# Turning the latent heads' queries and keys by 32x32 block transposes and transfers instead of on TensorE, with the attention rounds in another order

## The reference, cut to what is computed

```
proj = n @ w_in
c_q, c_kv, k_pe, r_q, r_k, r_v, r_g = split(proj)
q = (rms_norm(c_q) @ w_uq)        # 8 heads x (64 plain + 32 rotated)
kv = (rms_norm(c_kv) @ w_ukv)     # 8 heads x (64 key + 64 value)
s = einsum(q_nope, k_nope) + einsum(rope(q_pe), rope(k_pe))
a = softmax(s * MLA_SCALE) @ v    # latent heads
r = retention_group(r_q, r_k, r_v, r_g)   # decayed scores, no softmax
h = h + concat(a, r) @ w_o
```

## Time and profile before

| | us |
|---|---|
| median of 3 runs | 1026.04 (1025.88 to 1027.49) |
| profiled execution | 1026.88 |
| its span, first to last instruction | 1025.1 |
| TensorE busy | 1015.6 (99%) |
| VectorE busy | 686.6 (67%) |
| ScalarE busy | 564.4 (55%) |
| GpSimd busy | 140.7 (14%) |

### The profile page before, as it was taken

One profiled execution on the slowest core, in us unless ns is written; L12 is line 12 of the kernel. 1 busy time (PEld: TensorE's weight loads), 2 busy tenths in 40 slices (PEclk: granted clock), 3 DMA queues, 4 the chain that ended last, 5 costly groups with the idle time before them and its releaser, 6 DMA issues.

```text
span 1025.1 us, 14271 instructions
## 1 busy us (share of the span) xinstructions
PE 1015.6 (99%) x4764; PEld 836.6 (82%) x4764; DVE 686.6 (67%) x1041; ACT 564.4 (55%) x923; POOL 140.7 (14%) x219
## 2 busy tenths in 40 slices
PE   9999999999999999999999999999999999999997
PEld 6999888888877778888888888888887688888886
DVE  6777865646688985656568565656788785655643
ACT  6665654545567764444556454454676854454542
POOL 1001450000143253000014000000400221000002
PEclk9999999999999999999999999999999999999999
DMA  9574567566643467657576665757653455756551
GB/s 369 187 243 168 195 222 240 183 221 206 207 144 125 145 226 251 224 195 239 180 232 195 231 214 191 244 175 243 200 184 124 146 184 182 245 184 231 195 168 46
DMA packets 109694, 204.61 MB, mean 200 GB/s; under 512 B 57472, under 2 KB 62992, under 8 KB 109648
## 3 DMA queue, kind: packets, MB, share of 16 engines
q1 hardware_dynamic: 107472, 198.55, 57.9%
q0 software_dynamic: 1888, 5.17, 1.6%
q10 hardware_dynamic: 288, 0.31, 0.1%
HBM read 187.20 MB, written 1.05 MB: 184 GB/s over the span
## 4 chain that ended last, share of the span: by engine, by line
PE 93%; DVE 3%; DMA 1%; ACT 1%; SPq 1%; POOL 0%; issue 0%; POOLq 0%; DVEq 0%; ACTq 0%
PE pG L2185 16%; PE pG L2177 16%; PE pG L2181 16%; PE pD L2177 11%; PE pD L2181 11%; PE pD L2185 11%; PE pG L2158 2%; PE pG L2160 1%; PE pG L2164 1%; PE pT L2194 1%; DVE w_low L1735 1%; DMA h<-in_x 1%; PE pD L2158 1%; PE pD L2164 1%; PE pD L2160 1%; PE pT L2379 1%
## 5 line engine op out<-in xcount | busy, mean ns | idle before, releaser
L1735 DVE TENSOR_TENSOR w_low<-raw,w_high 128x1024 fp32r<-128x1024 f32 x339 | 408.9, 1226 | 181.4 <-ACT w_high L1424 171.3
L1424 ACT ACTIVATE w_high<-raw 128x1024 fp32r<-128x1024 f32 x340 | 353.5, 1056 | 192.1 <-PE pG L2185 134.4
L2177 PE MATMUL pG<-w_high,xTh 128*128 128x512 f32 x712 | 219.8, 390 | 0.0
L2185 PE MATMUL pG<-w_low,xTh 128*128 128x512 f32 x712 | 219.4, 389 | 0.2 <-DVE w_low L1735 0.2
L2181 PE MATMUL pG<-w_high,xTl 128*128 128x512 f32 x712 | 219.3, 389 | 0.0
L2185 PEld LDWEIGHTS pG<-w_low,xTh 128*128 128x128 f32 x712 | 133.6, 188 | 28.3 <-DVE w_low L1735 0.6
L2181 PEld LDWEIGHTS pG<-w_high,xTl 128*128 128x128 f32 x712 | 133.5, 188 | 28.0 <-DVE xTl L1795 0.2
L2177 PEld LDWEIGHTS pG<-w_high,xTh 128*128 128x128 f32 x712 | 133.2, 188 | 27.5
L1531 ACT ACTIVATE gate<-pG,stat 128x256 f32<-128x256 f32 x102 | 48.4, 474 | 151.8 <-PE pG L2185 135.9
L2177 PE MATMUL pD<-w_high,aTh 128*128 128x512 f32 x348 | 107.8, 391 | 0.0
L2181 PE MATMUL pD<-w_high,aTl 128*128 128x512 f32 x348 | 107.4, 390 | 0.1
(11 more groups left out here) (318 smaller groups left out, 1113.0 us busy)
## 6 DMA issues: line engine op xcount, KB each, us to landing
raw<-in_stream SPq DMA_DIRECT2D x340, 512.0 KB, 4.3
aF<-aB SPq DMA_DIRECT2D x320, 32.0 KB, 2.5
post<-in_posts POOLq DMA_DIRECT2D x5, 512.0 KB, 5.9
early<-in_stream SPq DMA_DIRECT2D x4, 512.0 KB, 12.5
xF<-hg SPq DMA_DIRECT2D x32, 64.0 KB, 2.5
xF<-hg POOLq DMA_DIRECT2D x32, 64.0 KB, 2.2
h<-in_x SPq DMA_DIRECT2D x2, 512.0 KB, 11.6
first_w<-in_opening SPq DMA_DIRECT2D x2, 384.0 KB, 4.2
```

Source lines behind the costliest of these rows:

```text
L1424: sc.activation(w_high[:, slot(static):slot(static) + CHUNK], raw_of(static), ACT.Copy).then_inc(w_high_done, 1)
L1735: ve.tensor_tensor(w_low[:, slot(static):slot(static) + CHUNK], raw_of(static), w_high[:, slot(static):slot(static) + CHUNK].bitcast(F32), ...
L2177: pe.matmul(dst, ah, w_high[:, where:where + n], start=start, stop=False)
L2185: mm = pe.matmul(dst, ah, w_low[:, where:where + n], start=False, stop=stop)
```

## The change

MT is gone. In its place MB(t) turns 32x32 blocks on VectorE, queries into `post` (free at that time), keys into `mk_turned` (over `junk`), and MV(t) moves them with 8 transfers, 4 from SyncE and 4 from GpSimd. The features of a head are spread over three blocks of 32, and the columns of `w_uq` and `w_ukv` are put in that order on the host. RV(t) is split: queries from SyncE, keys from GpSimd. The first scores stand two chunks later, behind products (3,1,0) and (3,1,1); in a round the order is MS(v), MPT(v-2), ME(v), MN(v-1), one chunk, MPV. Refills of rounds 1 and 3 move to round 7 and behind it.

```
@@ walk_latent
     refill(step, freed, 2)
-    step("MT", 0)
+    step("MB", 0)
+    step("MV", 0)
     refill(step, freed, 2)
     step("KPE", 1)
...
     step("U", 1)
+    step("MB", 1)
+    step("MV", 1)
     step("exp_table",)
     step("RROPE", 1, 0)
     refill(step, freed, 1)
     freed += [C_U, C_U + 1, C_U + 2]
     projects(3, 0, range(2))
-    step("MT", 1)
     refill(step, freed, 1)
     behind_maxima = freed.pop(0) + RING
     step("high", behind_maxima)
     projects(3, 0, range(2, 4))
+    step("RB", 0, 0)
+    project(3, 1, 0)
+    project(3, 1, 1)
     step("MS", 0)
-    step("low", behind_maxima)
     step("ME", 0)
-    step("RB", 0, 0)
-    step("RB", 0, 1)
-    beside = [(3, 1, c) for c in range(4)] + [(4, 0, c) for c in range(4)] + [(4, 1, 0)]
-    project(*beside.pop(0))
-    project(*beside.pop(0))
+    beside = [(3, 1, 2), (3, 1, 3)] + [(4, 0, c) for c in range(4)] + [(4, 1, 0)]
     for v in range(1, 8):
+        step("MS", v)
+        if v >= 2:
+            step("MPT", v - 2)
+        step("ME", v)
         step("MN", v - 1)
-        step("MS", v)
-        if v in (1, 3):
+        if v == 1:
+            step("low", behind_maxima)
+        if v == 7:
             refill(step, freed, 1)
-        step("ME", v)
+        project(*beside.pop(0))
         if v in (3, 5, 7):
             step("MPV", v - 3)
             step("MPV", v - 2)
-        project(*beside.pop(0))
-        step("MPT", v - 1)
         if v == 2:
-            step("VC", 0)
+            step("RB", 0, 1)
+        if v == 3:
+            step("RROPE", 1, 1)
         if v == 4:
             step("RV", 0)
-            step("RROPE", 1, 1)
+            step("VC", 0)
...
         if v == 7:
             step("RV", 1)
-            step("VC", 1)
...
     step("MN", 7)
-    refill(step, freed, 2)
+    step("VC", 1)
+    refill(step, freed, 3)
     project(4, 1, 1)
+    step("MPT", 6)
     step("MPT", 7)
@@ places
-        mqT = place("mqT", [QK, 2, MLA_HEADS, P], F32)
+        mqT = place("mqT", [QK, 2, MLA_HEADS, 4, 32], F32)
-        mkT = place("mkT", [QK, MLA_HEADS, SEQ], F32)
+        mkT = place("mkT", [QK, 2, 4, MLA_HEADS, 32], F32)
@@ SyncE; GpSimd has the same with a in range(2, 4) and m_sent
+            def MV(t, ph):
+                sp.wait_ge(mB_ready, 2 * t + 1)
+                for a in range(0, 2):
+                    sp.dma_start(mqT[:, t, :, a, :], post[32 * a:32 * a + 32, 0:MLA_HEADS * QK]).then_inc(m_moved, 16)
+                sp.wait_ge(mB_ready, 2 * t + 2)
+                for a in range(0, 2):
+                    sp.dma_start(mkT[:, t, a, :, :], mk_turned[32 * a:32 * a + 32, :]).then_inc(m_moved, 16)
@@ SyncE, retention
             def RV(t, ph):
                 sp.wait_ge(ms_psum, 4 * (t + 1))
-                for part in range(2):
-                    sp.wait_ge(rB_ready, 2 * t + part + 1)
-                    for a in range(4):
-                        dst = rkT[:, t, :, a, :] if part else rqT[:, t, a, :, :]
-                        sp.dma_start(dst, block_turned(t, part)[32 * a:32 * a + 32, :]).then_inc(rT_moved[t], 16)
+                if t == 1:
+                    sp.wait_ge(rqT_moved, 64)
+                sp.wait_ge(rB_ready, 2 * t + 1)
+                for a in range(4):
+                    sp.dma_start(rqT[:, t, a, :, :], block_turned(t, 0)[32 * a:32 * a + 32, :]).then_inc(rqT_moved, 16)
@@ VectorE
+            def MB(t, ph):
+                ve.wait_ge(mqk_ready, 2 * t + 2)
+                if t == 1:
+                    ve.wait_ge(m_moved, 64)
+                    ve.wait_ge(m_sent, 64)
+                ve.transpose(post[:, 0:MLA_HEADS * QK], mq[:]).then_inc(mB_ready, 1)
+                ve.wait_ge(u_out, 4 * t + 3)
+                ve.transpose(mk_turned[:], mk[:]).then_inc(mB_ready, 1)
@@ TensorE
                 if v == 0:
-                    for r in range(2):
-                        pe.wait_ge(mqT_ready, 2 * r + 2)
-                        pe.wait_ge(mkT_ready, 2 * r + 2)
+                    pe.wait_ge(m_moved, 128)
+                    pe.wait_ge(m_sent, 128)
+                    pe.wait_ge(u_out, 8)
...
-                    mm = pe.matmul(pG[v % 2][:, SEQ * x:SEQ * (x + 1)], mqT[:, t, hd, :], mkT[:, hd, :],
+                    mm = pe.matmul(pG[v % 2][:, SEQ * x:SEQ * (x + 1)], mqT[:, t, hd, :, :].rearrange("p a j -> p (a j)"), mkT[:, :, :, hd, :],
```

More of the change, by code:

```diff
@@ L1200, in finish @@
                 sp.wait_ge(out_stored, 80)
-            steps = dict(start=start, low=low, low_half=low_half, R=refill, V=V, spread=spread, RV=RV, finish=finish)
+            steps = dict(start=start, low=low, low_half=low_half, R=refill, V=V, spread=spread, MV=MV, RV=RV, finish=finish)
             walk(sp, lambda name, *a, ph=None: steps[name](*a, ph) if name in steps else None)
@@ L1646, in U @@
                     copied(2, 1)
-            def MT(t, ph):
-                sc.wait_ge(mT_psum, 2 * t + 1)
-                for half in range(2):
-                    sc.activation(mqT[:, t, 4 * half:4 * half + 4, :],
-                                  (pG, pT)[half][0][0:QK, :].rearrange("p (a r) -> p a r", a=4), ACT.Copy).then_inc(mqT_ready, 1)
             def ME(v, ph):
@@ L2020, in RB @@
                 ve.wait_ge(rrope_done[t], part + 1)
+                if (t, part) == (0, 0):
+                    ve.wait_ge(mB_ready, 4)
                 ve.transpose(block_turned(t, part), rqk[t][:, 512 * part:512 * part + 512]).then_inc(rB_ready, 1)
@@ L2522, in RS @@
                     pe.wait_ge(mp_ready, 16)
-                    for t in range(2):
-                        pe.wait_ge(rT_moved[t], 128)
+                    pe.wait_ge(rqT_moved, 128)
+                    pe.wait_ge(rkT_moved, 128)
                 else:
@@ L2651, in weight_chunks @@
         if i == 2:
-            parts.extend(np.concatenate([uq[P * k:P * (k + 1)], pad], axis=1) for k in range(2))
-            parts.append(ukv.transpose(0, 2, 1, 3).reshape(P, CHUNK))
+            turned_q = uq.reshape(Q_RANK, MLA_HEADS, 3, 32).transpose(0, 2, 1, 3).reshape(Q_RANK, -1)
+            turned_k = ukv[:, :, 0].reshape(KV_RANK, MLA_HEADS, 2, 32).transpose(0, 2, 1, 3).reshape(KV_RANK, -1)
+            parts.extend(np.concatenate([turned_q[P * k:P * (k + 1)], pad], axis=1) for k in range(2))
+            parts.append(np.concatenate([turned_k, ukv[:, :, 1].reshape(KV_RANK, -1)], axis=1))
         cols = w_in[:, LATENT + 512 * i:LATENT + 512 * (i + 1)]
```

73 lines of the change are left out of this document (39 added, 34 removed).

## The result

The changed kernel takes 1032.69 us in the median of 5 executions (1030.72 to 1035.38); the kernel before takes 1026.04 (5 executions, 1025.52 to 1027.49). The ratio is 1.0066, with a 95% interval of 1.0053 to 1.0078: slower by 6.7 us. The profiled execution took 1030.72 with a span of 1028.9.

The account below looks back on a forecast made before the run. TensorE, busy in 99% of the span, was taken as the bound. Terms -3.50 - 1.03 - 0.3 + 0.93 + 2.6 + 0.36 + 0.25 + 1.0 = +0.31 us on 1026.04 gave 1026.4, range 1023.8 to 1030.0.

Parts of the forecast that it names:

- 1, TensorE's transposes go: Latent mixer: 32 PE transposes of MT and the slower chunks behind them leave TensorE, -3.50 us.
- 2, X(2,1,0) waits for ScalarE: Behind the removed MT(0), TensorE must wait for ScalarE to empty the product's PSUM bank: +0.93 us, called certain.
- 4, MS(0) waits: First latent scores wait for the turned queries' and keys' transfers behind a DMA backlog: +2.6 us, from 1.3 to 3.9.
- C, half clock behind it: Rival, chance 0.07: after a 3 us wait TensorE's clock falls to 1.2 GHz, +3.4 us on the forecast: 1029.8.
- 6, RS(0): First retention scores: the old 1.03 us wait goes, a new one of 0.5 to 2.0 comes, taken as 1.0.
- 5, MPV, MPT(0), MPT(7): Rounds of the latent mixer: MPV's 0.3 us wait goes; waits of 0.36 at MPT(0) and 0.25 at MPT(7) come.
- Parts 1 to 3: The third: VectorE's four new block transposes take 0.94 us each, about 0.5 more per half; query block turned at 765.9.
- The price by pieces: DMA engine cost of turned transfers: 0.69 us per query transfer in 128-byte pieces, 0.36 at most per key transfer.
- the 0.6 us from last byte to semaphore: Estimated delay added after the turned transfers' last byte, giving all there at 773.05.
- the rule on queues: For MV's split over SyncE and GpSimd: a second queue saves issue time and none of the DMA backlog.
- MV(0) would not bind: First half's transfers land near 764, so MB(1)'s wait for them is not binding by over 1 us.
- B: Rival, chance 0.20: DMA backlog is not filled up, MS(0) waits 3.9 to 7 us; +3.2, 1029.2.

Follow-up runs that it names:

- e12: Kernel before, unedited, profiled a second time: span 1024.3 us, no wait at RS(0).
- e11: Changed kernel, unedited, profiled again: span 1028.3 us, wait at MS(0) 3.4; its series gave a median of 1031.55 against 1025.56 for the kernel before.
- e14: Changed kernel, unedited, fourth profiled execution: span 1029.5 us, wait at MS(0) 3.7, 6.8 us at half clock.
- e13: Changed kernel, unedited, third profiled execution: span 1031.0 us, wait at MS(0) 5.1, 6.8 us at half clock.
- e2: Changed kernel with the turned queries written in pieces of 1 KB instead of 128 bytes (scores read mixed-up queries): 1031.27 us, a wait of 3.9.
- e10: Changed kernel with all eight transfers of MV per half issued from SyncE, none from GpSimd: 1033.65 us, a wait of 6.9.
- e3: Changed kernel with four weight loads issued behind the second half's turned keys instead of ahead: 1034.26 us, waits of 2.8 and 4.5.
- e9: Kernel before with all of the change except the block transposes and their transfers (MT stays on TensorE): 1026.96 us against 1025.56, ratio 1.0012.
- e4: Kernel before with MS(0) made to wait for three small transfers sent one after the other by GpSimd: 1032.04 us against 1026.16.
- e1: Changed kernel with 14 useless matmuls of 512 columns in front of the first score matmuls: 1029.23 us.
- e7: Changed kernel with MS(0) two projections later, those two taken from behind the last round: 1032.70 us (1028.31 to 1038.29).
- e15: Kernel before with MS(0) made to wait for two small transfers sent one after the other by GpSimd: 1029.38 us, profiled wait 2.0.
- e8: Kernel before with only the rotated keys' transfers moved to GpSimd's queue: 1026.06 us against 1025.85, ratio 1.0003.
- e6: Changed kernel without the second half's four query transfers per queue, all scores reading the first half's queries: 1026.54 us, a wait of 1.0.

## Why the prediction was wrong, point by point

Forecast was +0.31 us; the median came out at +6.65, outside the range. The step that failed is the slower clock behind the wait at MS(0), which the sum put at nothing; the wait itself, RS(0) and the end of the span make up the rest. The terms, in the profiled executions, against the second profile of the kernel before (e12) where the earlier trace rows misled:

| step | predicted | measured |
|---|---|---|
| 1, TensorE's transposes go | -3.50 | -3.4 |
| 2, X(2,1,0) waits for ScalarE | +0.93 | +0.94 |
| 4, MS(0) waits | +2.6 (1.3 to 3.9) | +3.2, +3.4, +3.7, +5.1 in four executions |
| C, half clock behind it | 0 (3.4 at 0.07) | +1.8, +1.7, +2.8, +2.9 |
| 6, RS(0) | -1.03 + 1.0 | +0.7 to +0.9 |
| 5, MPV, MPT(0), MPT(7) | +0.31 | +0.1 (what is left in e11) |
| not seen: the end of the span | 0 | +0.9 |

From the start of the first product behind 742 us to the start of the last matmul the kernel before takes 274.4 (e12), the changed one 277.8 (e11): +3.4, and with the end +4.3. The medians' +6.0 and +6.7 lie between e14 (+4.8, with the end +5.8) and e13 (+6.3, with the end +7.2), the profiled executions with more wait and more half clock. That the unprofiled ones differ in the same way is inferred from their mean clocks of 0.993 to 0.996; their rows are not seen.

**Parts 1 to 3 held.** The transposes, X(2,1,0) and the block transposes of 0.94 to 0.98 came as worked out. Their start at 766.0 (predicted 765.9) agrees in part by chance, since this execution was 0.7 us late already at 742. Counted from the first product behind 742 us, they start 22.1 to 24.1 us on in the four profiles, where the forecast had 23.0.

**Part 4 held in kind and was low in size.** The backlog was there: the share of the DMA engines is 1.04 to 1.07 from 757 to 772 in the four profiles. Three of the four waits lie inside the range of 1.3 to 3.9, all four above the 2.6. The prices were read off wrongly: the two windows of the earlier trace rows were taken to hold four transfers each, but 78 GB/s over 2.7 us and 92 over 3.5 are 211 and 322 KB, 3.2 and 4.9 transfers of 64 KB. Windows of the same trace that hold four each, 795.0 to 798.0 (share 0.41, 92 GB/s) and 798.0 to 800.75 (0.57, 94), give 0.31 us in 512-byte pieces and 0.39 in 128-byte ones. By these a half costs up to 4 x 0.46 + 4 x 0.59 = 4.2 us, and the part's own sum gives a wait of 3.9. The price by pieces, which the prediction held to be what would upset the sum most, mattered little (e2). No row shows the 0.6 us from last byte to semaphore. The 5.1 us landing that the part holds beside the rule on queues is that of a load on one queue; what a second queue is worth is first seen in e10.

The part also said that MV(0) would not bind. It did not bind MB(1) by its landing, but in e13 a weight load that landed late, ahead of U(1), held up the second batch, a path that the part did not look at.

**Rival C is the step that failed.** It was priced (3.4) and given 0.07, for the sole reason that the trace held no such wait. But the forecast itself put a wait of 2.6 us there, and a second one at RS(0). The runs show the clock at 0.50 behind all eight profiled waits of 3.0 us and more and behind one of 2.0, at a cost of 1.7 to 2.9 us in the changed kernel. The Trainium skill, "TensorE: Matmul & The Clock Gate", section "Part 1: The HAM clock gate (the "warmup" mystery)", says that an idle TensorE falls to half rate. These nine waits agree; one of 2.8 (e3) did not bring it. With C as a part of the forecast, the sum is +2.0 to +3.2, inside the range still. B and C were priced as alternatives, though C follows from the very wait that B lengthens. Both together, at the prediction's own prices, are 0.31 + 2.9 + 3.4 = +6.6; that this meets the median is in part luck, since it leaves out RS(0) and the end of the span.

**Part 6 counted a gain that was not there.** The -1.03 came from one landing of 3.6 us in one execution. Three later profiles of that arrangement have none. One profile shows what can happen, not what a median holds; a worst landing of 3.6 beside a median of 2.2 in the same line was the hint. The wait that the part added came as worked out, 0.7 to 0.9 for 1.0. The view names no releaser for it ("issue"), but SyncE's last transfer was issued at 802.7 and landed 2.5 us on, at 805.2, when RS(0) starts.

**The cost of the order** (e9, +1.4) was forecast at about zero. Parts 5 and 6 without the gain that never was come to +1.3 (0.31 + 1.0).

## What to carry to other kernels

A step that takes work off the engine that sets the time and leaves a wait in its place must be charged the wait and the slower clock behind it. Here a wait of 4.3 us cost 5.9 (e4), and filling a wait with useless matmuls made the kernel 2.3 to 3.5 us faster (e1). Cover has to come from work that is free to move: e7 moved it from another place that needed it.

Before a wait in one profile is booked as a gain, look at the spread of the landing behind it, or take a second profile. And look at what a transfer put into a full stretch has beside it: a weight load that landed 2 us later (e13) held up the engines that make the next batch.

## What the runs showed of the hardware that was not expected

- The clock fell behind waits of 2.0 (e15), 3.0, 3.2, 3.6, 3.9, 4.3, 4.5, 4.9 and 6.9 us, and stayed up behind one of 2.8 (e3) and those of 0.4, 1.0 and 1.5. Behind these waits it fell 2.3 to 4.9 us after TensorE had run dry, in some executions before the work resumed and in some after, and stayed at 1.2 GHz for 3.4 us or for 6.8; in e10, with the longest wait, for 10. In e7 it fell with no wait above 1.6: at 802.4, 0.6 us behind two waits of 1.6 and 0.6 that lie 0.7 us apart, and ahead of one of 0.9. The 4.5 of e3 began 3.2 us behind the end of that run's wait of 2.8, so it does not stand for itself. The length of a wait alone does not tell its cost.
- The span ends later behind the start of the last matmul the more transfers GpSimd's queue has carried, though the instructions and transfers of the end are the same: 6.6 us with none added (before, twice), or 2 or 3 (e15, e4), 6.8 with 8 (e8, e9, e10), 7.3 with 14 (e6), 7.4 to 7.5 with 16 (nine profiles of the changed kernel and its variants). The added time lies behind the last output transfer: it is issued 3.4 us on and lands in 2.2 in the kernel before and in the changed one, and the span ends 1.0 and 1.9 us behind that. No row shows what it is; that it goes with the queue's count is seen in e10, which moved eight from GpSimd to SyncE and ended at 6.8.
- In the stretch of the second batch's transfers from one place in SBUF to another (769 to 772 us) the engines moved 233 to 286 GB/s at a share of 1.0 to 1.2, in six profiles (the changed kernel's four, e1, e2). In the 3 us ahead of it, when weight loads issued from 760 on were landing, it was 385 to 404 at 1.0 to 1.1.
- Pieces of 128 bytes or 1 KB made little difference to the landing in such a burst (medians of 4.6 and 4.7 against 4.2 and 4.4 us for the second batch's queries). They do to the issuing queue: 0.79 against 0.53 us each on GpSimd. And they do to the engines' busy time: at 92 and 94 GB/s the share was 0.41 with 512-byte pieces and 0.57 with 128-byte ones (kernel before, 795 to 800.75).
